# A two-block transformer kernel on one core: norms by a diagonal product, modulation shared by two engines, a three-pass recurrent output, and expert weights in longer rows

## The chip, the core and the metric

The kernel is one program on one core of a Trainium2 chip. TensorE multiplies (PE in the profile; PEld is its weight load), VectorE (DVE), ScalarE (ACT) and GpSimd (POOL) work on tiles, and SyncE (SP) issues the loads. The metric is the device time of one execution in microseconds; less is better.

## The reference

Two blocks run one after the other on 256 tokens of width 1024, beside a context of 256 tokens, all in float32. The first block has an attention layer and a recurrent layer (HGRN2), each followed by a gated feed-forward network (FFN) with a convolution of width 3. The second has dilated and windowed attention and a mixture of 32 experts. What the change touches:

```python
hx = rms_norm(x, norm1_g[layer]) * (1.0 + sc1) + sh1          # before each mixer, with scale and shift from c
x = x + g1 * yx
hx2 = rms_norm(x, norm2_g[layer]) * (1.0 + sc2) + sh2          # before each FFN
# HGRN2: projections q, forget gates fw and bw, input, gate of 8 heads of 128
q = silu(q);  f = lb + (1 - lb) * sigmoid(fl)
o = rms_norm(o_fw + o_bw, o_gain) * silu(gate)                 # the norm is over the 128 of each head
y = o @ w_out
# experts
hdn = gt * sigmoid(1.702 * gt) * (up + 1.0);  y_e = hdn @ w_down[e] + b_down[e]
```

## The kernel before, in words

Tokens lie on partitions in four tiles of 128: tiles 0 and 1 are x, tiles 2 and 3 the context. The residual stream is `xr`. A projection needs its input turned, with the 1024 channels on partitions in 8 chunks, in `hT` and its like.

**Passes.** A float32 product on TensorE is slow. So most products are made in three passes of a faster float type: input and weights are each split in a high part (rounded, by a ScalarE copy) and a low part (the rest, by a VectorE subtraction), and high x high, low x high and high x low are summed in one bank. Two products were still plain float32: the first half of the recurrent queries, `("hq", 0)`, by `move`, and the recurrent output projection `wo1`, by `project`.

**Order of the work.** Each engine runs its own program in the order in which it is written. `psum_ready` counts finished banks; a list (`add`, from line 349 on) fixes in which order the 8 banks are used and whether ScalarE or VectorE empties each. `bank` (TensorE) waits until the reader of the bank eight groups earlier has freed it; `take` (ScalarE, VectorE) waits for the bank. After every ScalarE or VectorE instruction `do` waits for it. `await_next` waits for the next count of a semaphore. SyncE loads weights in units of 2 MB into a ring of three slots, in the order of a list (line 858), each unit after its slot's last user. Slot 2 is also used as scratch, so some units may use slots 0 and 1 only.

**Passage into the first FFN.** `enter_first` (VectorE) adds the projected tile to `xr` by `gated_add` (L2060, L2061), then `rms` makes square sum (L1984), reciprocal (L1988, after ScalarE's square root L1470) and the normed tile `xn` (L1989). TensorE turns it (`turn`, L936). ScalarE modulates the 8 chunks of 128 columns (`norm_turn`, L1490) into `modp` and copies them rounded to `hT_high` (L1494), and VectorE subtracts (`split_tokens`, L2067). The FFN's products wait for all low parts. Weights are rounded by `weights_high` (L1555) and their low part made by `low_part` (L809). The first bank of the FFN is read at L1571.

**Passage into the recurrent layer.** After the last `gated_add` of the FFN, `rms` runs over four tiles, ScalarE modulates all of them into `hT` (`norm_turn`, L1490) and copies the whole to `hx_high` (L1732). VectorE makes the forget gates' lower bounds (L2317 to L2326) and `hx_low` (L2328). The 20 half units of 256 columns follow: `half_high` (L1756) rounds one, VectorE makes its low part (L2350), TensorE uses it, `take_half` empties the banks. `log_forget` (L1780) takes logarithms; `keys_and_sums` (L2335, L2341, L2344) makes running sums. `context_decay` (L1798) and `decay_keys` (L2359) begin the recurrence.

**Recurrence and readout.** For each direction d and half of the heads b, seven levels run through subtraction (VectorE, L2367), exponentials (ScalarE, L1840, L1841), scaling (VectorE, L2388, L2389), products (TensorE) and masks. The last of four passes is (1, 1). Its output is added to `ro` (L2420). Then head norms (L2425 to L2431) run over both tiles of 1024 columns, with the gain row and the gate `rg` multiplied in, then `turn`, ScalarE copies to `hT` (L1504), `wo1` in float32, `gated_add`, and the second FFN, entered as above but with two tiles only, and with its weights rounded after them.

**Experts.** A load of an expert's weight is split in two runs of 2 MB, 16 KB a partition each. Gate, up and down weights have one buffer each; `gate` of expert e+1 is issued when `gate` of e has been multiplied, and so on (L760, L768, L773). Expert 0 is loaded ahead. GpSimd reorders the tokens once (L815) to fit the channels that each partition gets.

## Time and profile before

| | us |
|---|---|
| median of 3 runs | 2708.53 (2706.02 to 2712.92) |
| profiled execution | 2706.67 |
| its span | 2704.8 |
| busy: TensorE, VectorE, ScalarE | 2398.8, 976.9, 787.2 |

The chain of work that ended last is 72% TensorE, 12% DMA, 7% VectorE and 6% ScalarE of the span. A busy time is the sum of an engine's instructions and says nothing of what they wait for; the chain names at each moment what the rest waited for. In the rows below times are microseconds from the start of the span, and a number after x is a count.

### The profile page before, as it was taken

To read this page: it belongs to the slowest core of one execution; us is meant where nothing else is said; L and a number is where in the kernel's file an instruction comes from. 1 tells how busy PE (TensorE), PEld (TensorE's weight loads), DVE (VectorE), ACT (ScalarE), POOL (GpSimd) and SP (SyncE) were. 2 spreads that over 40 slices of the span, in tenths; PEclk is the share of its full clock that TensorE was granted. 3 is DMA by queue.
4 is the path that set the end of the run, shared out by engine and by line. 5 is a ranking of instruction groups with operands and counts; after the bars stand their busy time and mean duration, and the time that the engine had idled before them with its cause. 6 is when DMAs were issued, how large, how long until landed. Compare 5 with 4: busy or idle time off the path is not lost.

```text
span 2704.8 us, 32119 instructions
## 1 busy us (share of the span) xinstructions
PE 2398.8 (89%) x13052; PEld 1574.8 (58%) x13052; DVE 976.9 (36%) x1557; ACT 787.2 (29%) x1242; POOL 4.2 (0%) x6
## 2 busy tenths in 40 slices
PE   6998879999979976579999888799999999999995
PEld 4844857886768966459889873434333333333332
DVE  5465433433332677646543442511111111111112
ACT  4376342322152544235434440110111111011110
POOL 0000000000000000000000000000000000000000
PEclk9999989999979988789999979799999999999998
DMA  8267135322023200225554302699999999999993
GB/s 321 94 233 234 63 109 184 97 94 94 25 96 108 100 1 1 94 89 180 192 190 164 123 1 83 276 424 429 427 429 428 424 430 421 427 429 417 421 429 146
DMA packets 142267, 603.57 MB, mean 223 GB/s; under 512 B 6513, under 2 KB 51825, under 8 KB 117457
## 3 DMA queue, kind: packets, MB, share of 16 engines
q1 hardware_dynamic: 142160, 602.10, 56.8%
q8 instruction: 74, 1.21, 0.2%
q14 instruction: 33, 0.26, 0.0%
HBM read 601.03 MB, written 1.05 MB: 223 GB/s over the span
## 4 chain that ended last, share of the span: by engine, by line
PE 72%; DMA 12%; DVE 7%; ACT 6%; issue 2%; SPq 0%; ACTq 0%; DVEq 0%
PE bank L902 70%; DMA arena<-in_b_up 10%; DMA ring<-in_ada_w 2%; DVE arena L2399 1%; ACT modp L1490 1%; PE bank L936 1%; ACT arena L1718 1%; ACT hT L1490 1%; ACT arena L1527 1%; PE bank L1119 0%; DVE modp L2389 0%; DVE xn L2388 0%; DVE xr L2061 0%; DVE xn L1984 0%; ACT modp L1465 0%
## 5 line engine op out<-in xcount | busy, mean ns | idle before, releaser
L902 PE MATMUL bank<-arena 128*64 128x512 f32 (+5 forms) x2896 | 601.2, 511 | 88.7 <-ACT arena L1934 25.7
L902 PEld LDWEIGHTS bank<-arena 128*64 128x64 f32 (+2 forms) x2896 | 287.6, 169 | 347.4 <-issue 260.7
L902 PE MATMUL bank<-ring,arena 128*64 128x512 f32 (+1 forms) x1632 | 394.9, 608 | 23.7 <-DMA arena<-in_b_up 21.3
L902 PE MATMUL bank<-hT_high,w_split 128*128 128x512 f32 (+1 forms) x1408 | 349.0, 339 | 18.2 <-issue 9.9
L902 PEld LDWEIGHTS bank<-ring,arena 128*64 128x64 f32 (+1 forms) x1632 | 141.0, 143 | 270.3 <-issue 260.1
L902 PEld LDWEIGHTS bank<-hT_high,w_split 128*128 128x128 f32 x1408 | 244.1, 191 | 47.8 <-issue 11.3
L902 PE MATMUL bank<-hT_low,w_split 128*128 128x512 f32 (+1 forms) x704 | 237.9, 338 | 0.0
L2536 DVE TENSOR_SCALAR arena<-bank 128x512 f32<-128x512 f32 x32 | 22.1, 692 | 548.8 <-PE bank L902 548.8
L902 PEld LDWEIGHTS bank<-hT_low,w_split 128*128 128x128 f32 x704 | 134.8, 192 | 14.5 <-issue 1.0
L809 DVE TENSOR_TENSOR w_split<-ring,w_split 128x1024 fp32r<-128x1024 f32 x88 | 107.8, 1225 | 27.6 <-ACT w_split L1555 25.9
L1555 ACT ACTIVATE w_split<-ring 128x1024 fp32r<-128x1024 f32 x88 | 93.4, 1062 | 62.5 <-PE bank L902 49.0
L2540 DVE TENSOR_SCALAR arena<-bank 128x512 f32<-128x512 f32 x32 | 22.1, 692 | 223.2 <-PE bank L902 223.2
L902 PE MATMUL bank<-ring,hT 128*128 128x512 f32 (+1 forms) x240 | 98.1, 570 | 2.9 <-ACTq L720 2.9
L1930 ACT ACTIVATE arena<-arena 128x512 f32<-128x512 f32 x32 | 20.1, 629 | 245.9 <-DVE arena L2536 245.9
L1937 ACT ACTIVATE arena<-bank 128x512 f32<-128x512 f32 x32 | 19.1, 597 | 232.6 <-PE bank L902 232.6
L902 PE MATMUL bank<-down_high,hid_high 128*128 128x512 f32 x216 | 84.9, 393 | 0.0
L902 PE MATMUL bank<-down_low,hid_high 128*128 128x512 f32 x216 | 84.0, 389 | 0.0
L902 PE MATMUL bank<-down_high,hid_low 128*128 128x512 f32 x216 | 84.0, 389 | 0.0
L1921 ACT ACTIVATE arena<-bank 128x512 f32<-128x512 f32 x34 | 18.5, 595 | 208.4 <-PE bank L902 208.4
L902 PEld LDWEIGHTS bank<-ring,hT 128*128 128x128 f32 x240 | 44.5, 197 | 55.2 <-issue 51.3
L2350 DVE TENSOR_TENSOR hw_low<-ring,hw_high 128x2048 fp32r<-128x2048 f32 x18 | 41.3, 2293 | 96.7 <-ACT hw_high L1756 96.6
L902 PE MATMUL bank<-ring,cT 128*32 128x512 f32 x384 | 52.7, 672 | 24.1 <-DMA ring<-in_ada_w 24.1
(344 smaller groups left out, 3671.7 us busy)
## 6 DMA issues: line engine op xcount, KB each, us to landing
ring<-in_w_gate SPq DMA_DIRECT2D x64, 2048.0 KB
arena<-in_w_down SPq DMA_DIRECT2D x64, 2048.0 KB, 15.0
ring<-in_w_up SPq DMA_DIRECT2D x32, 2048.0 KB
arena<-in_w_up SPq DMA_DIRECT2D x32, 2048.0 KB
ring<-in_ada_w SPq DMA_DIRECT2D x24, 2048.0 KB, 8.1
ring<-in_ffn_w_up SPq DMA_DIRECT2D x44, 1024.0 KB, 7.9
ring<-in_w_in SPq DMA_DIRECT2D x11, 2048.0 KB, 7.9
ring<-in_ffn_w_down SPq DMA_DIRECT2D x10, 2048.0 KB, 7.7
```

What stands on the lines that cost most here:

```text
L809: then(eng.tensor_tensor(w[:, 1, :, g, :], raw, w[:, 0, :, g, :].bitcast(F32), ALU.subtract))
L902: return pe.matmul(o, l, r, start=start, stop=stop)
L936: m = pe.transpose(ps[:, i * P:(i + 1) * P], src(t)[:, k * P:(k + 1) * P], ident)
L1490: do(act.activation(o, ps[:, j * P:(j + 1) * P], ACT.Identity, bias=modT[:, l, 24 * i + k, v:v + 1], scale=coef[:, l, i, k, v:v + 1]), F i ...
L1527: do(act.activation(pr, pr, ACT.Exp, bias=st[:, 4 + r:5 + r], accum_out=st[:, 12 + r:13 + r]))
L1555: do(act.activation(w_split[fc % 2][:, 0, :, g, :], raw[:, :, g, fc % 2, :], ACT.Copy), w_high)
L1718: do(act.activation(PT0[:, c % 2, :], ps[:, :], ACT.Copy), F)
L1930: act.activation(sg[:, :], hm[:, :], ACT.Sigmoid, scale=1.702).then_inc(sg_ready, 1)
L2350: do(TT(hw_low[:, slot_of[unit_no[key]], :, 256 * z:256 * z + 256], raw, hw_high[j % 2][:, :, :].bitcast(F32), ALU.subtract), hw_low_ready)
L2399: do(dve.copy_predicated(rA[:, t, :, :], m, ps), F)
L2536: dve.tensor_scalar(hm[:, :], PS[0][:, :], 7.0, None, ALU.min).then_inc(hm_ready, 1)
L2540: link(dve.tensor_scalar(um[:, :], PS[1][:, :], 7.0, -7.0, ALU.min, ALU.max))
```

## The change

1. **Norms by matmul with a diagonal.** `rms` is gone. ScalarE squares and sums a tile itself (`square_sum`) and takes the root; VectorE makes the reciprocal and a 128 x 128 diagonal matrix with it (`inverse_norm`, in the dead rope table). TensorE multiplies `xr` by the diagonal (`pair`, float32), which turns and scales in one product. The products of two tiles stand side by side, 256 columns of one chunk.
2. **Pairs modulated by two engines.** `split_pair`: banks q = 0, 2 are modulated by ScalarE, q = 1, 3 by VectorE, in calls of 256 columns; ScalarE rounds, VectorE makes the low parts. On entry to an FFN, the first products wait for low parts chunk by chunk. In `enter_first` two tiles go together; in the second FFN all weights of the first two columns are rounded before the pair.
3. **Recurrent layer.** The first query half joins the three-pass halves; `("h1", 1)` is turned after the first of them. In ScalarE's loop a half is rounded one iteration later (`half_high(j + 1)` instead of `j + 2`). Norms of tiles 0 and 1 come before the last adds. The lower bounds are made at the start. The gain row is multiplied into `rg` ahead of the recurrence.
4. **Head norms head by head.** ScalarE squares 128 columns at a time with a sum, the first four heads inside pass (1, 1). VectorE scales four heads at a time.
5. **`wo1` in three passes**, with weights rounded inside pass (1, 1), and low parts after the readout.
6. **Expert loads.** Gate and up are each one load of 4 MB, 32 KB a partition, with the token order to fit.

```diff
+            def pair(tag, v):
+                for t in range(2 * v, 2 * v + 2):
+                    await_next(xn_ready)
+                for q in range(4):
+                    key = ("pair", tag, v, q)
+                    ps = bank(key)
+                    for c in range(2):
+                        k = 2 * q + c
+                        for t in range(2 * v, 2 * v + 2):
+                            m = mm(ps[:, c * SEQ + t % 2 * P:c * SEQ + t % 2 * P + P], xr[:, t, k * P:(k + 1) * P],
+                                   diag[:, t, :], True, True)
+                    close(m, key)
...
-                await_next(x_low, 2 * T)
+                x_before = 8 if l else 0
...
+                                if j == 0 and i == 0 and g == 0 and n % 6 == 0:
+                                    pe.wait_ge(x_low, x_before + 2 * T - 4 + k // 2 + 1)
...
                 for t in ALL:
...
+                    if b and t == 3:
+                        pair(("f", 0), 0)
+                    project_split("wo0", b, t, wo_high, o_high, o_low, wo_low_ready)
+            pair(("f", 0), 1)
             ffn(0, NT)
...
-            turn("h1", ALL, lambda t: xn[:, t % 2, :], lambda t: await_next(xn_ready))
-            await_next(hT_ready)
-            s = unit(("hq", 0))
-            for i in range(4):
-                m = move(("hq", i), s, i * P, P, SEQ)
-            release(m)
-            await_next(hx_low_ready)
+            pair("h1", 0)
             for j, (key, z) in enumerate(HALVES):
+                if j == 1:
+                    pair("h1", 1)
                 s = unit(key) if z == 0 else slot_of[unit_no[key]]
                 await_next(hw_low_ready)
+                pe.wait_ge(hx_low_ready, 4 if j < 2 else 8)
...
# ScalarE
+            def square_sum(t):
+                await_next(res_ready)
+                do(act.activation(xn[:, 1, :], xr[:, t, :], ACT.Square, accum_out=stat[:, t:t + 1]))
+                do(act.activation(stat[:, t:t + 1], stat[:, t:t + 1], ACT.Sqrt, bias=C("eps6")[:, 0:1], scale=1.0 / D),
+                   std_ready)
...
+            def split_pair(tag, v, l, i, high, high_sem, low_sem):
+                tok = slice(v * SEQ, (v + 1) * SEQ)
+                for q in range(4):
+                    n = lows[low_sem.name] = lows.get(low_sem.name, -1) + 1
+                    if q % 2 == 0:
+                        ps = take(("pair", tag, v, q))
+                        if n >= 2:
+                            act.wait_ge(low_sem, n - 1)
+                        for c in range(2):
+                            k, cut = 2 * q + c, slice(c * SEQ, (c + 1) * SEQ)
+                            do(act.activation(modp[:, 0, cut], ps[:, cut], ACT.Identity,
                                               bias=modT[:, l, 24 * i + k, v:v + 1], scale=coef[:, l, i, k, v:v + 1]),
+                               F if c else act_step)
+                    else:
+                        await_next(mod_ready)
+                    do(act.activation(high[:, 2 * q:2 * q + 2, tok],
+                                      modp[:, q % 2, :].rearrange("p (k c) -> p k c", k=2), ACT.Copy), high_sem)
...
+            await_next(coef_ready)
+            square_sum(0)
+            square_sum(1)
+            pe_past(("down", 0, NT - 1, 1))
             half_high(0)
+            split_pair("h1", 0, 1, 0, hx_high, hx_high_ready, hx_low_ready)
+            square_sum(2)
+            square_sum(3)
             half_high(1)
-            take_queries(0, 4)
-            await_next(lb_ready)
             for j in range(len(HALVES)):
-                if j + 2 < len(HALVES):
-                    half_high(j + 2)
+                if j and j + 1 < len(HALVES):
+                    half_high(j + 1)
                 take_half(j)
+                if j == 0:
+                    split_pair("h1", 1, 1, 0, hx_high, hx_high_ready, hx_low_ready)
                 if j in LOGS:
                     log_forget(*LOGS[j])
...
+                        if (d, b) == (1, 1):
+                            if n in (1, 2):
+                                head_squares(0, n - 1)
+                            if n >= 4:
+                                wo1_part(n - 4)
...
# VectorE
+            def inverse_norm(t):
+                await_next(std_ready)
+                do(dve.reciprocal(stat[:, t:t + 1], stat[:, t:t + 1]))
+                do(dve.tensor_scalar(diag[:, t, :], ident, stat[:, t:t + 1], None, ALU.mult), xn_ready)
...
                 for t in range(T):
+                    if l == 0 and t == 2:
+                        inverse_norm(0)
+                        inverse_norm(1)
                     for h in range(2):
                         gated_add(("down", l, t, h), h, t, GATE[(l, 1)])
...
             keys_and_sums(1, 1)
+            for t in XS:
+                await_next(rg_ready, 2)
+            for t in XS:
+                v = rg[:, t, :].rearrange("p (h c) -> p h c", h=HG)
+                do(TT(v, v, ROW("og").unsqueeze(1).broadcast_to((P, HG, P)), ALU.mult))
...
+            normed(0)
+            normed(1)
+            for h in range(2):
+                for t in XS:
+                    cut = (slice(None), slice(4 * h, 4 * h + 4), slice(t * P, (t + 1) * P))
+                    ps = take(("turn", "o1", t, h))[:, :].rearrange("p (k q) -> p k q", k=4)
+                    await_next(o1_high_ready)
+                    do(TT(o1_low[cut], ps, o1_high[cut].bitcast(F32), ALU.subtract), F)
+                    signal(o1_low_ready)
+            for j in range(4):
+                wo1_rest(j)
             ffn(1, XT)
...
# SyncE, expert loads
             for j in range(2):
                 slot_free(j)
-                sp.dma_start(moe_slot[j], runs(a["w_gate_2"], e, j)).then_inc(gate_landed, 16)
+            sp.dma_start(ring[:, 0:2, :].rearrange("p a b -> p (a b)"), whole(a["w_gate_2"], e)).then_inc(gate_landed, 16)
...
-                sp.dma_start(moe_slot[2 + j], runs(a["w_up_2"], e, j)).then_inc(up_landed, 16)
+            sp.dma_start(up_w[:, :, :].rearrange("p a b -> p (a b)"), whole(a["w_up_2"], e)).then_inc(up_landed, 16)
```

`head_squares(b, t)` is four Squares of 128 columns with a sum; `wo1_part(j)` a rounding copy of 128 x 2048; `wo1_rest(j)` its low part; `normed(b)` a reciprocal and two products of 512 columns for each of two tiles.

## Rows read from the trace of the kernel before

**Rows 1.** The page: busy times, and two lines of the 40 slices

```profile
PE 2398.8 (89%) x13052; PEld 1574.8 (58%) x13052; DVE 976.9 (36%) x1557; ACT 787.2 (29%) x1242; POOL 4.2 (0%) x6
...
DMA  8267135322023200225554302699999999999993
```

**Rows 2.** Windows: length, busy (count) by engine, granted clock, DMA share, GB/s

```profile
745.00:757.00 12.00, 7.84 (x32) 6.27 (x32) 7.71 (x16) 4.51 (x12) 0.00 (x0) 0.50 1.05 389
...
770.00:775.00 5.00, 5.00 (x15) 4.07 (x16) 0.00 (x0) 4.94 (x4) 0.00 (x0) 0.62 0.00 0
...
1213.00:1217.00 4.00, 4.00 (x35) 4.00 (x35) 3.26 (x5) 2.40 (x3) 0.00 (x0) 1.00 1.09 365
...
1740.00:2656.00 916.00, 867.33 (x4154) 349.06 (x4152) 127.70 (x266) 100.51 (x155) 0.00 (x0) 0.99 1.00 425
```

**Rows 3.** Chain of waits, 275 to 390 us: start, length, what

```profile
287.45 34.82 PE bank L902 x288
...
356.57 0.70 DVE hT_low L2067
```

**Rows 4.** Groups of ScalarE and VectorE, 318 to 358 us: busy, mean ns, idle before

```profile
L1490 ACT ACTIVATE modp<-bank,modT,coef 128x128 f32<-128x128 f32 x32 | 14.6, 458 | 1.1
L1494 ACT ACTIVATE hT_high<-modp 128x512 fp32r<-128x512 f32 x8 | 5.0, 630 | 0.3
...
L2067 DVE TENSOR_TENSOR hT_low<-modp,hT_high 128x512 fp32r<-128x512 f32 x8 | 5.5, 692 | 14.3 <-ACT hT_high L1494 14.3
```

**Rows 5.** Timeline, single instructions of four stretches: start, length, engine, line

```profile
16.74 1.28 ACT L1470 ACT_TABLE_LOAD   x1 [13.40 <-DMA rows<-in_rows]
18.04 1.27 ACT L1470 ACTIVATE stat<-stat,const 128x1 f32<-128x1 f32 x4
...
142.72 0.19 ACT L1709 ACTIVATION_READ_ACCUMULATOR arena<-arena,stat 128x1 f32 x1
...
364.76 0.78 ACT L1571 ACTIVATE xn<-bank,cols 128x512 f32<-128x512 f32 x1 [6.11 <-PE bank L902]
...
2007.57 3.84 PE L902 MATMUL bank<-arena,xn 128*128 128x128 f32 x32
```

**Rows 6.** Timeline of SyncE's issues and of ScalarE, 716 to 812 us

```profile
740.55 89.22 SPq L858 DMA_DIRECT2D ring<-in_hgrn_w_in  x5
...
753.99 15.69 ACT L1490 ACTIVATE hT<-bank,modT,coef 128x128 f32<-128x128 f32 x32
...
785.92 0.38 ACT L1739 ACTIVATE arena<-bank 128x256 f32<-128x256 f32 x1 [3.07 <-PE bank L902]
```

**Rows 7.** DMA issues by line: count, KB each, median us from issue to landing

```profile
ring<-in_hgrn_w_in SPq DMA_DIRECT2D x10, 2048.0 KB, 7.9
```

**Rows 8.** Timeline of VectorE and ScalarE, 880 to 992 us

```profile
913.16 3.36 ACT L1780 ACTIVATE xr<-arena,stat 128x512 f32<-128x512 f32 x4
...
923.23 2.29 DVE L2350 TENSOR_TENSOR hw_low<-ring,hw_high 128x2048 fp32r<-128x2048 f32 x1
...
947.24 2.30 DVE L2335 TENSOR_SCALAR hT<-hT,stat 128x512 f32<-128x512 f32 x4
...
955.38 0.17 DVE L2344 COPY stat<-last_sums 128x4 f32<-128x4 f32 x1
...
959.86 1.22 DVE L2359 TENSOR_TENSOR xr<-xr,arena 128x1024 f32<-128x1024 f32 x1 [0.93 <-ACT xr L1798]
```

**Rows 9.** Timeline of VectorE, ScalarE, and the chain's projection, 1069 to 1205 us

```profile
1097.11 0.69 DVE L2388 TENSOR_TENSOR xn<-arena,xn 128x512 f32<-128x512 f32 x1 [2.50 <-ACT xn L1841]
...
1123.84 0.69 DVE L2420 TENSOR_TENSOR arena<-arena,bank 128x512 f32<-128x512 f32 x1 [1.21 <-PE bank L902]
...
1144.36 30.16 PE bank L902 x64
...
1191.09 4.33 ACT L1555 ACTIVATE w_split<-ring 128x1024 fp32r<-128x1024 f32 x4
1198.31 0.56 ACT L1571 ACTIVATE xn<-bank,cols 128x256 f32<-128x256 f32 x1 [2.90 <-PE bank L902]
```

More of the change, by code:

```diff
@@ L536, in program @@
                     add(("ro", d, b, t), "dve" if d else "act")
-        plan_turn("o1", XS)
+        for h in range(2):
+            for t in XS:
+                add(("turn", "o1", t, h), "dve")
         for b in range(2):
@@ L999, in ffn @@
                 if l:
-                    turn(("f", l), range(T), lambda t: xn[:, t % 2, :], lambda t: await_next(xn_ready))
-                await_next(x_low, 2 * T)
+                    pair(("f", l), 0)
+                x_before = 8 if l else 0
                 for j in range(FC // 2):
@@ L1557, in ffn @@
             def ffn(l, T):
[L1558 to L1563 removed]
+                enter(l)
                 n = T * P
```

345 lines of the change are left out of this document (201 added, 144 removed).

## The prediction

> **What bounds the kernel now.** I read the page first: its busy times, and the DMA line of its 40 slices [rows 1]. TensorE is busy 89% of the span, but DMA is at 9 tenths or more from slice 27 on, so two regimes follow one another. The windows say what rules the second [rows 2]: from 1740 to 2656 us the DMA share is 1.00 at 425 GB/s, which is the expert stage (expert 0 was loaded ahead, 31 experts of 12.6 MB follow). The other two windows give the same stream at shorter rows. So the expert stage costs its bytes; what is saved ahead of it arrives undiminished at the end, since its clock starts with the first gate product, and nothing saved on TensorE inside it would count. The first regime (0 to 1725 us) I read by the chain of waits. It runs along TensorE except at the passages between blocks, where it goes from VectorE to ScalarE and back: 322.4 to 357.3 us [rows 3], 740 to 786 us [rows 6], and 1123.8 to 1198 us [rows 9]. The change sits in these three, in the end of the recurrent projection [rows 8] and in the expert loads.
>
> **Prices of the new operations.** ScalarE modulates 128 columns in 0.458 us now [rows 4]; 512 columns of the same form take 0.78 us [rows 5], so 256 lie between, by the line 0.57 us. The rounding copy is 0.63 us and the low part 0.69 us [rows 4]. A norm by diagonal is 16 f32 products of 128 columns; the same shape in the expert stage, 16 products recorded as x32, takes 3.84 us [rows 5] at full clock. At the other level, 0.50 in the 745 to 757 window [rows 2], it would be up to twice that. VectorE's modulation of 256 columns I take at 0.5 us (bounds 0.35 and 0.69, half and whole of a 512-column operation [rows 4]). A Square with its sum is shown nowhere: 1.08 us for a 1024-column ScalarE pass (4.33 for four [rows 9]) plus the accumulator read, 0.19 and its gap [rows 5], gives 1.35, and 0.57 at 128 columns; bounds 0.6 (a 512-column pass) and 2.6 (with a table load of 1.28 [rows 5] before it).
> One pair of tiles then goes as follows, T being the first bank: ScalarE q0 2 x 0.6 + 0.65 = 1.85; copy of q1 to 2.5; low parts of q0, q1 at 2.7 and 3.4; q2 may start at 2.7; low parts of q2, q3 at 5.3 and 6.0. So 6 us for a pair, where before ScalarE alone took 32 x 0.458 + 8 x 0.63 = 19.7 us for four tiles [rows 4], 9.8 for two.
>
> **Passage 1, attention to the first FFN.** Before: the last low part ends at 357.3 and the first FFN product follows; its first bank closes at 364.7 [rows 3, 5]. After: pair 0 is put in front of the last projection tile on TensorE (done before at about 335.5, behind the other transposes), so that tile ends near 337.4, 3.84 us of pair against the transposes it replaces. VectorE by then has pair 0 and the weights' low part behind it and adds the tile to 339.1. Square and Sqrt to 340.8, diagonal to 341.3, first bank 342.3, low parts at 345.0, 345.7, 347.6 and 348.3. The first FFN bank may now start at the first low part and waits chunk by chunk, so it is bound by the last low part plus six products: it closes at 352.5 (351 if nothing stalls, 354 if the pair runs at the low clock). Gain 12 us (10.5 to 13.5). Queued behind the new waits on TensorE is only the FFN itself.
>
> **Passage 2, FFN to the recurrent projection.** Before: after the adds VectorE makes four norms in turn, then 15.7 us of modulation, then a copy; TensorE starts the first query half at 769.8 and has done with it at 785.9 [rows 6]. After: Square and Sqrt of tiles 0 and 1 run beside the adds, but VectorE waits some 2 us for them in between, so its adds end near 744.8, 4 us after TensorE's last product. New is a wait ahead of everything on ScalarE: the first query weights, issued at 740.6 and landing 7.9 to 8.1 us later [rows 6, 7], hold `half_high(0)` to 748.8, and pair 0's modulation queues behind it. The pair's norm product at 740.4 is hidden by that. Rounding to 750.7, VectorE's low part of the weights (2.29 us [rows 8]) to 753.1, then q1, so the last low part comes at 758.1. The first half, 48 products of 256 columns at 34.82 / 288 = 0.12 us [rows 3], is 5.8 us, plus 1.9 because the clock stands at its lower level after the idle time and rises late (0.62 over the 5 us from 770 [rows 2], 0.38 x 5 = 1.9), to 765.7; pair 1's norm 3.8 to 769.6, the second query half 5.8 to 775.4. Beside it pair 1 ends at 772.7, and ScalarE's next weights only then: 773.9, low part 776.2. The first forget-gate product thus starts at 776.2 instead of 785.9: gain 9.5 us (6 to 12).
>
> **End of the projection.** Two things speak against the change here. The weights' rounding is now ordered behind the previous half's evacuation, and behind the logarithms (3.36 us, after a table load [rows 8, 5]): the last half but two is rounded 1.2 + 1.3 + 3.4 = 5.9 us later. VectorE's keys and sums (947.2 to 955.5, 8.2 us a group) wait for it in order, and its chain that ended at 955.5 ends at 957.0 on the old time scale. Then the gain row multiplied into the gate, 2 x 1.25 = 2.5 us, stands before the first decay. `decay_keys`, at 959.86 now released by ScalarE's exponentials [rows 8], starts at 962.7: 3 us lost (0 to 5).
>
> **Last recurrent pass and readout.** Squares of the first heads (4 x 0.57 = 2.3 us of ScalarE each tile) and four weight roundings (1.95 us each) enter a pass in which VectorE at one place waits 2.5 us for ScalarE [rows 9]. The second squares delay the scaling at 1097.1 by 0.6 us; the second to fourth roundings make ScalarE late by another 1.0. Lost 1.6 us (0 to 4).
> Then the readout. Before: second add 1124.5, norm chain to 1139.8, transposes, f32 projection 30.2 us from 1144.4, adds to 1176.0, norms, modulation of two tiles to 1191.1, four weight roundings, FFN from 1193.6, its first bank at 1198.3 [rows 9]. After, with the 1.6 in it: add to 1126.2; first half of heads scaled by 1129.3, second by 1132.4; transposes beside them; low parts to 1135.7; four weights' low parts at 2.3 each follow in order, the first two by 1138.0 and 1140.3. TensorE: 192 products of 256 columns at 0.12 us = 23.1, from 1138.0, plus 1.9 for the clock = 1163.0 (before 1174.5). Add to 1164.6, Square and Sqrt 1166.3; the four roundings of up weights (4.33 [rows 9]) now stand BEFORE the modulation on ScalarE: 1170.6. VectorE comes from their low parts at 1172.4; low parts of the pair 1174.0 to 1177.4; first FFN bank 1178.8. The low parts of the weights, before after the pair, are then paid. Gain of the whole: 1198.3 - 1178.8 = 19.5 us, the 1.6 counted (14 to 23).
> The forget gates' lower bounds, moved to the start, hide there: ScalarE waits 13.4 us for the first parameters [rows 5], and the moved exponential with its table load is 1.5 us.
>
> **Expert loads.** Gate and up come as one 4 MB load of 32 KB rows instead of two of 16 KB. Order and releases stay: the product waited for all loads of its weight already, and all three of expert 0 are issued together. Only bytes per second can change. From the windows [rows 2] a row costs an engine 44.9 ns (1 KB, 365 GB/s), 84.2 (2 KB, 389), 617 (16 KB, 425): a line with 6 to 8 ns per row. One less per 32 KB is 0.45 to 0.66% on two thirds of 916 us: 2.8 to 4 us. I take 3.5; bounds 0 and, the other way, rival 3. The Trainium skill (DMA: Bandwidth & Descriptors, "Where 436 GB/s comes from") puts the ceiling of the ports at 435 GB/s. If all of the distance from 425 to 435 were cost per row, 16 KB would take 602 ns and 15 more, and the estimate by that page would be 7 us instead of 3.5. The 1 and 2 KB windows give half of those 15 ns at most, so the rows decide.
>
> **Sum.** 12 + 9.5 - 3 + 19.5 + 3.5 = 41.5. Some thirty handoffs of about 0.07 us that the timelines leave out take back 2: gain 39.5. The profiled execution took 2706.7 us (span 2704.8); the median of the runs is 2708.5, 1.8 above it. 2706.7 - 39.5 = 2667.2, or 2669 by the median; I say 2668.
>
> **Rivals.**
> 1. The stream does not notice the longer rows: 3.5 less, 2671.5. For it: 425 is the mean with dips, and the line rests on windows of a few us. It differs too little to be told from the forecast by the total, only by the stage.
> 2. The shared modulation ping-pongs: each half of `modp` is single, so ScalarE waits for VectorE's low part and VectorE for ScalarE's copy. If a pair costs what it did (9.8 us, not 6), three pairs on the path cost 3 x 3.8 = 11.4, and if half of the readout's gain goes the same way (the four weights' low parts wait behind everything on VectorE), 8 more (half of 19.5 - 3.8): 2667.2 + 19.4 = 2687. For it: VectorE's idle before each low part, 14.3 us in eight, is of this kind [rows 4]. Against: VectorE now carries half of the modulation.
> 3. Slower than before: rows at a 32 KB pitch make the 16 DMA engines collide. All 16 read addresses 128 KB apart instead of 64. At the 2 KB windows' 389 GB/s the 260 MB of gate and up would take 668 instead of 611 us: +57, less 36 for the rest (39.5 without the 3.5): 2667.2 + 3.5 + 57 = 2728. It decides from 6% loss of rate on, 425 to 400 GB/s. No row shows pitch as a cost: the 1 and 2 KB rows come at pitches of 20 to 22 KB and lie on the line.
> 4. Squares between exponentials call for their own table: two extra loads of 1.28 us in each of two places, about half hidden: +2.5. For it: no row shows a Square between exponentials. Against: it is the only kind of ScalarE work here that would. The Trainium skill (ScalarE: Activation LUTs, "What ACT_TABLE_LOAD costs") adds a drain of about 1.4 us to every switch; this trace does not show it, the Sqrt at 18.04 starts 0.02 us after its load's end [rows 5], and with the rule the rival would cost twice as much. It lies inside my range.
>
> **How the numbers follow.** Forecast with rivals 1 and 4 in it, 72%, itself 2660 to 2677; rival 2, 17%; still better than forecast, because the first FFN banks hide more, 6%; rival 3 or another loss of that size, 3%; other losses 2%. Leaving out a tenth at each end: 2655 to 2688. About 0.3% (8 us) is what a measurement can tell. Faster 0.95, same 0.02, slower 0.03.
>
> **What would show it.** Right: first FFN product near 345 and first bank by 354; ScalarE idle to the landing of the first query weights and the first forget product about 21 us earlier than 785.9; VectorE going into `decay_keys` without a wait for ScalarE; projection with 192 products of 0.12 us; 31 experts in 912 us at 427 GB/s. Wrong: low parts more than 7 us after a pair's first bank, table loads among the squares, DMA share below 1.00 or under 420 GB/s in the expert stage.

## The result and the profile after

The changed kernel takes 2666.12 us (median of 4 runs, 2664.47 to 2668.32) against 2709.27 us (4 runs, 2706.02 to 2712.92) of the kernel before: ratio 0.984, 95% interval 0.9828 to 0.9852, 43 us or 1.6% faster. I had said 2668 (2655 to 2688). The page after, in its rows that answer to [rows 1]:

```profile
span 2662.6 us, 32524 instructions
PE 2390.5 (90%) x13292; PEld 1587.2 (60%) x13292; DVE 984.0 (37%) x1574; ACT 792.6 (30%) x1247; POOL 4.2 (0%) x6
...
PEclk9999999999989988899999898899999999999997
...
DMA packets 133053, 603.61 MB, mean 227 GB/s; under 512 B 5488, under 2 KB 50800, under 8 KB 116432
```

The busy times have hardly moved (TensorE -8, VectorE +7, ScalarE +5 us): what went is idle time between engines, and the lower clock that follows it. So the page can't say where; stages can. I cut each trace at landmarks that all kernels have (a bank's first read, a product, a load). "Others" are the traces of the experiments below in which that stage is not edited; a stage is timed from its own first landmark. The first stage holds a small edit: the forget gates' lower bounds stand there now.

| stage, us | before (others) | changed (others) | gain | forecast |
|---|---|---|---|---|
| start to first add of the attention's projection | 293.7 (294.8 to 299.7) | 296.0 (294.3 to 301.5) | -2.3 | 0 |
| passage 1, to the first FFN bank read | 71.1 (71.0 to 71.5) | 60.4 (60.1 to 60.5) | 10.7 | 12 |
| first FFN, to its first down add | 366.4 | 366.4 | 0 | 0 |
| passage 2 and projection, to its last bank read | 224.6 (224.6 to 225.5) | 217.3 (217.3 to 217.9) | 7.3 | 9.5 |
| to the first decay product | 4.1 | 7.8 | -3.6 | -3 |
| four recurrent passes | 155.2 (154.5 to 155.5) | 154.4 (156.0 to 157.2) | 0.8 | -1.6 |
| readout, to the second FFN's first bank | 83.3 (83.2 to 83.3) | 62.6 (62.7) | 20.6 | 21.1 |
| second FFN, to its last gate bank read | 120.9 | 120.9 | 0 | 0 |
| its down products, second attention, router, to expert 1's gate load | 420.3 (420.3) | 415.2 (407.7 to 421.5) | 5.0 | 0 |
| experts, to the end | 965.3 (964.4, 965.5) | 961.6 (959.7 to 961.9) | 3.7 | 3.5 |
| sum | | | 42.2 | 41.5, less 2 for handoffs |

The sum is right to 3 us, but that closeness is partly luck: 5 us of it come from a stage that the change doesn't touch, and the first stage, 2.3 us longer in this trace, lies within its scatter in the others. The rows that carry the stages follow; times are start and duration, the bracket is the idle time before and what ended it.

Passage 1, timeline of ScalarE, VectorE, ScalarE again, and TensorE's norm products of the first and the second pair (answers to [rows 3 to 5]):

```profile
320.50 1.06 ACT L1533 ACTIVATE xn<-xr 128x1024 f32<-128x1024 f32 x1 [27.48 <-DVEq L743]
321.47 0.18 ACT L1533 ACTIVATION_READ_ACCUMULATOR xn<-xr 128x1 f32 x1
321.67 1.28 ACT L1534 ACT_TABLE_LOAD   x1
322.96 0.30 ACT L1534 ACTIVATE stat<-stat,const 128x1 f32<-128x1 f32 x1
...
343.89 0.29 DVE L2079 TENSOR_SCALAR rope<-const,stat 128x128 f32<-128x128 f32 x1
348.14 1.12 DVE L2089 TENSOR_SCALAR modp<-bank,coef,modT 128x256 f32<-128x256 f32 x2 [3.97 <-PE bank L929]
352.15 1.42 DVE L2095 TENSOR_TENSOR hT_low<-modp,hT_high 128x512 fp32r<-128x512 f32 x2 [0.16 <-ACT hT_high L1555]
...
346.41 1.16 ACT L1550 ACTIVATE modp<-bank,modT,coef 128x256 f32<-128x256 f32 x2 [2.83 <-PE bank L929]
356.34 0.78 ACT L1633 ACTIVATE xn<-bank,cols 128x512 f32<-128x512 f32 x1 [1.37 <-PE bank L929]
...
330.18 3.74 PE L929 MATMUL bank<-rope,xr 128*128 128x128 f32 x32
...
344.27 6.49 PE L929 MATMUL bank<-rope,xr 128*128 128x128 f32 x32 [4.61 <-DVE rope L2079]
```

The new prices are close to the forecast: a Square with its sum takes 1.17 us from its start to the next instruction (1.35 forecast), 256 columns 0.58 on ScalarE (0.57) and 0.56 on VectorE (0.5). The Square comes ahead of the table load and needs none. From the diagonal (343.89) the pair takes 9.7 us to its last low part at 353.57 (352.15 + 1.42). TensorE's 16 norm products, recorded as x32, took 3.74 us for the first pair and 6.49 for the second, which stands behind 4.61 us of idle time.

Passage 2, chain of waits (start, duration, what), and VectorE's low part of the weights that the first forget-gate product needs (answers to [rows 6, 7]):

```profile
732.14 7.83 DMA ring<-in_hgrn_w_in
...
740.07 1.92 ACT hw_high L1814
742.01 2.30 DVE hw_low L2456
...
749.08 0.70 DVE hx_low L2095
...
750.03 17.97 PE bank L929 x128
768.00 1.66 issue
```
```profile
767.27 2.29 DVE L2456 TENSOR_TENSOR hw_low<-ring,hw_high 128x2048 fp32r<-128x2048 f32 x1 [1.25 <-ACT hw_high L1814]
```

The chain calls the last 1.66 us "issue", time in which it sees no wait. But the forget-gate product starts at 769.66, 0.10 us after that low part ends (769.56), and the program makes it wait for it.

End of the projection, timelines of ScalarE and VectorE (answers to [rows 8]):

```profile
917.62 3.36 ACT L1839 ACTIVATE ring<-hT,stat 128x512 f32<-128x512 f32 x4
921.01 1.92 ACT L1814 ACTIVATE hw_high<-ring 128x2048 fp32r<-128x2048 f32 x1
...
923.03 2.29 DVE L2456 TENSOR_TENSOR hw_low<-ring,hw_high 128x2048 fp32r<-128x2048 f32 x1 [1.62 <-ACT hw_high L1814]
942.04 2.48 DVE L2493 TENSOR_TENSOR arena<-arena,rows 128x1024 f32<-128x1024 f32 x2
947.79 1.23 DVE L2498 TENSOR_TENSOR xr<-xr,arena 128x1024 f32<-128x1024 f32 x1
```

Readout, chain of waits (answers to [rows 9]):

```profile
1120.06 0.70 DVE o_low L2587
1120.90 2.31 DVE hw_low L2577
1123.45 25.34 PE bank L929 x192
...
1150.39 1.16 ACT xn L1533 x2
1151.89 1.06 ACT w_split L1622
1153.05 1.24 DVE w_split L836
...
1162.32 0.70 DVE hT_low L2095
```

### The profile page after: what moved, and what is told of

Its sections match the earlier page's. It is cut to its first block, busy times and chain, and to the rows that moved or that the text cites. A ratio compares the mean times of both kernels' runs of the same rounds, so it can differ in the third digit from the quotient of the medians.

```text
span 2662.6 us, 32524 instructions
## 1 busy us (share of the span) xinstructions
PE 2390.5 (90%) x13292; PEld 1587.2 (60%) x13292; DVE 984.0 (37%) x1574; ACT 792.6 (30%) x1247; POOL 4.2 (0%) x6
## 2 busy tenths in 40 slices
DMA packets 133053, 603.61 MB, mean 227 GB/s; under 512 B 5488, under 2 KB 50800, under 8 KB 116432
## 4 chain that ended last, share of the span: by engine, by line
PE 73%; DMA 12%; DVE 7%; ACT 5%; issue 2%; SPq 0%; ACTq 0%; DVEq 0%
PE bank L929 72%; DMA arena<-in_b_up 10%; DMA ring<-in_ada_w 1%; DVE arena L2538 1%; ACT arena L1781 1%; DMA ring<-in_attn_w_in 0%; ACT arena L1586 0%; PE bank L963 0%; PE bank L1182 0%; ACT arena L2030 0%; ACT modp L1522 0%; ACT w_split L1622 0%; DVE xn L2527 0%; DVE modp L2528 0%; PE bank L1441 0%
## 5 line engine op out<-in xcount | busy, mean ns | idle before, releaser
L929 PE MATMUL bank<-arena 128*64 128x512 f32 (+6 forms) x2384 | 479.3, 491 | 92.5 <-ACT arena L2030 25.7
L929 PEld LDWEIGHTS bank<-arena 128*64 128x64 f32 (+2 forms) x2384 | 240.7, 172 | 281.0 <-issue 190.7
L929 PE MATMUL bank<-ring,arena 128*64 128x512 f32 (+1 forms) x1120 | 269.5, 596 | 1.2 <-DMA arena<-in_b_gate 0.3
L929 PE MATMUL bank<-up_w,arena 128*64 128x512 f32 x1024 | 235.0, 613 | 19.3 <-DMA arena<-in_b_up 19.3
L929 PEld LDWEIGHTS bank<-ring,arena 128*64 128x64 f32 (+1 forms) x1120 | 101.5, 142 | 163.5 <-issue 154.3
L929 PEld LDWEIGHTS bank<-up_w,arena 128*64 128x64 f32 x1024 | 79.0, 140 | 174.0 <-issue 174.0
L929 PE MATMUL bank<-hx_high,hw_high 128*128 128x512 f32 (+1 forms) x192 | 69.5, 362 | 16.0 <-DVE hx_low L2095 14.3
```

What stands on the lines that cost most here:

```text
L929: return pe.matmul(o, l, r, start=start, stop=stop)
```

## Experiments

Each is timed against the kernel before on its own chip, whose medians there lie between 2708.9 and 2709.9 us; differences to the changed kernel's median compare runs made at different times and on several chips. For effects of a few us the stages of one trace each decide, since totals carry the spread of the first and the untouched stages. All edits are to the changed kernel unless said otherwise.

**rows16 and before_rows32: the expert loads alone, taken away and added.**

```
-            sp.dma_start(ring[:, 0:2, :]..., whole(a["w_gate_2"], e)).then_inc(gate_landed, 16)
+                sp.dma_start(moe_slot[j], runs(a["w_gate_2"], e, j)).then_inc(gate_landed, 16)
```

> The changed kernel, with the expert loads of gate and up back at two runs of 16 KB rows each (and the tokens in the order that goes with them). The profiled execution of the changed kernel takes 961.6 us from the issue of expert 1's gate to its end, the kernel before 965.3. Theory (each DMA engine pays 6 to 8 ns per row): this kernel returns to 965.1 us (964.5 to 965.8), all 16 KB windows at 425 GB/s, and nothing ahead of the expert stage moves; total 3.5 us above the changed kernel. Rival (the stream does not notice the longer rows, and the 3.7 us between the two kernels are scatter): 961.6 within 1 us.

> The kernel before, with nothing but the expert loads of gate and up as one run of 32 KB rows each. From the issue of expert 1's gate to the end it took 965.3 and 964.4 us in two traces with 16 KB rows, 964.4 in the changed kernel with 16 KB rows, and 959.7 to 961.6 in seven traces with 32 KB rows. Theory (the rows alone do it): 960.4 us (959.5 to 961.7), and all stages ahead as in the kernel before; total 4.4 us less. Rival (it needs the rest of the change, the order or the phase in which the stage is entered): 964 to 965.5.

Windows over the expert stage of the kernel before, the changed kernel, rows16 and before_rows32 (after the length: busy times and instructions of the five engines, granted clock, DMA share, GB/s):

```profile
1739.47:2704.80 965.33, 889.73 (x4260) 359.19 (x4256) 145.74 (x292) 104.66 (x162) 0.00 (x0) 0.98 0.96 406
```
```profile
1701.01:2662.60 961.59, 889.59 (x4260) 358.36 (x4256) 145.69 (x292) 104.67 (x162) 0.00 (x0) 0.98 0.95 407
```
```profile
1706.06:2670.50 964.44, 889.73 (x4260) 359.20 (x4256) 145.71 (x292) 104.66 (x162) 0.00 (x0) 0.98 0.96 406
```
```profile
1744.22:2704.50 960.28, 887.85 (x4260) 358.14 (x4256) 145.70 (x292) 104.65 (x162) 0.00 (x0) 0.98 0.95 408
```

16 KB rows: 964.4 to 965.5 in four traces of three kernels; 32 KB rows: 959.7 to 961.9 in ten traces. Both ways, and with everything else of the change or nothing, the longer rows bring the gain: 4.3 us between the means (964.9 and 960.6). 31 experts have 2 x 128 rows fewer each, 496 for each of 16 engines: 8.6 ns per row if all of it is theirs, above my 6 to 8. But the loads are halved with the rows. The page of the kernel before has

```profile
DMA packets 142267, 603.57 MB, mean 223 GB/s; under 512 B 6513, under 2 KB 51825, under 8 KB 117457
```

against 133053 and 5488 after: besides the 32 x 256 rows some 1020 packets under 512 B are gone, 16 for each load saved. What belongs to the row and what to the load no run separates. Totals: rows16 2671.46 (ratio 0.9855, 0.9835 to 0.9875); before_rows32 2705.13 against 2709.89 (0.998, 0.9969 to 0.9991).

**wo1_f32: the readout's projection without three passes.**

```
-                    project_split("wo1", b, t, wo1_high, o1_high, o1_low, wo1_low_ready)
+            await_next(hT_ready)
+            project("wo1", XS)
```

> The changed kernel, with the recurrent output projected in plain float32 from transposed heads, as before, and without the eight roundings and low parts that three passes need; head norms, norm by diagonal and shared modulation stay. In the changed kernel TensorE starts the projection at 1123.5, 3.4 us after its last operand low part, because the weights' first low part stands in between, runs 25.3 us, and the first FFN bank is read at 1164.9. Theory (the passes themselves bring little, the readout's gain of 20.6 us is the shorter chain of norms): start at about 1120.0, 30.2 us as before, end at 1150.2 against 1148.8, so the first FFN bank 1.4 us later (0 to 3), total +1.4. Rival (the three passes bring what their products save and more, since the roundings lie in free time): 5 us later or more.

Its chain of waits:

```profile
1120.22 0.60 ACT hT L1949
1120.92 30.33 PE bank L929 x64
```

From the last pass to the FFN bank 64.96 instead of 62.64: 2.3 us, in the theory's bounds; the rival falls. Of the readout's 20.6 us the three passes are worth 2.3; the other 18.3 are the shorter chain of norms and its order, the wait by chunk (wait_all, below) among them. And the 2.3 are not all profit, because the weights' roundings stand in the pass ahead. The last pass alone, in the kernel before, in wo1_f32 (squares, no roundings) and in rows16 (squares and roundings), with the lower clock at the same place of the pass in all three:

```profile
1074.49:1115.06 40.57, 28.53 (x200) 26.86 (x200) 30.29 (x37) 15.75 (x31) 0.00 (x0) 0.88 0.45 155
```
```profile
1061.51:1102.15 40.64, 28.60 (x200) 26.93 (x200) 30.29 (x38) 18.98 (x48) 0.00 (x0) 0.88 0.46 156
```
```profile
1068.26:1110.17 41.91, 28.56 (x200) 26.89 (x200) 30.29 (x38) 26.58 (x52) 0.00 (x0) 0.88 0.44 151
```

With roundings and this clock it takes 41.8 to 41.9 in six traces. So the squares cost nothing there and the roundings 1.2 us, and the three passes bring about 1.1 net, where the theory had 1.4. In the changed kernel's own trace, filler and weights_early the roundings are there too, but the pass has some 5 us less at the lower clock and takes 40.6. (Total 2660.88, ratio 0.9827, 0.9809 to 0.9845, lower than the changed kernel's although the edited stage is longer: its second attention and router took 407.7 instead of 415.2, see below.)

**one_engine: ScalarE modulates all chunks.**

```
-                    if q % 2 == 0:
-                        ps = take(("pair", tag, v, q))
+                    ps = take(("pair", tag, v, q))
...
-                        do(dve.tensor_scalar(modp[:, 1, cut], ps[:, cut], coef[:, l, i, k, v:v + 1],
```

> The changed kernel, with ScalarE modulating all eight chunks of every tile pair; VectorE only makes the low parts. Theory (two engines at once are what shortens a pair): ScalarE needs 4 x (1.16 + 0.63) = 7.2 us for a pair and the last low part comes 8 us after the first bank instead of 6, so about 1.8 us later at each of four places (both pairs ahead of the first FFN, the first ahead of the recurrent projection) and 0.6 at the readout, where ScalarE is held by weights anyway: total +5 us (3 to 7.5), of which +3.5 at the first FFN bank (356.3 in the changed kernel). Rival (VectorE is what a pair waits for, with 1.12 us of modulation and two low parts of 0.69 for two chunk pairs): nothing lost, total within 1 us.

Passage 1 took 62.4 (+2.0), passage 2 with the projection 219.9 (+2.6), the readout 63.4 (+0.7): 5.3 us, as the theory's sum, though passage 1 has less of it (2.0 where I had 3.5) and passage 2 more. Total 2673.86, ratio 0.9868 (0.9843 to 0.9894), +7.7.

**wait_all: the first FFN product waits for every low part.**

```
-                                if j == 0 and i == 0 and g == 0 and n % 6 == 0:
-                                    pe.wait_ge(x_low, x_before + 2 * T - 4 + k // 2 + 1)
+                                if j == 0 and i == 0 and g == 0 and n == 0:
+                                    pe.wait_ge(x_low, x_before + 2 * T)
```

> The changed kernel, with the first FFN product waiting for all low parts of its activations at both FFN entries, instead of chunk by chunk. In the changed kernel the last low part ends at 353.6 and the first bank is read at 356.3; at the second FFN 1163.7 and 1164.9. Theory: all 24 products now stand behind the last low part: 24 x 0.24 = 5.8 us of 512 columns and 24 x 0.12 = 2.9 of 256, so the banks are read at 359.5 (+3.2) and 1166.8 (+1.9) on the changed kernel's scale, more by up to 2 us each if TensorE's idle time takes its clock down. Total +5 (4.5 to 9). Rival (other waits of the first banks cover it, such as the convolution's chain or the weights): under 2 us in total.

Passage 1 64.9 (+4.5), readout 67.3 (+4.6), total 2675.1, ratio 0.9876 (0.9859 to 0.9894): +9.0, the upper end. That is more than the products behind the last low part (3.2 and 1.9 expected): the lower clock lasts 10.2 instead of 6.8 us in the one and 27.3 instead of 20.5 in the other. Waiting by chunk is worth a fifth of the whole change.

**order and gain_late: the two causes of the late decay product.**

```
+                if j == 1:
+                    half_high(2)
-                if j and j + 1 < len(HALVES):
-                    half_high(j + 1)
+                if j and j + 2 < len(HALVES):
+                    half_high(j + 2)
```
```
                             sub(d, b, n + 1)
+                        if (d, b, n) == (0, 1, 0):
+                            for t in XS:
+                                v = rg[:, t, :].rearrange("p (h c) -> p h c", h=HG)
+                                do(TT(v, v, ROW("og").unsqueeze(1).broadcast_to((P, HG, P)), ALU.mult))
...
-            for t in XS:
-                v = rg[:, t, :].rearrange("p (h c) -> p h c", h=HG)
-                do(TT(v, v, ROW("og").unsqueeze(1).broadcast_to((P, HG, P)), ALU.mult))
```

> The changed kernel, with ScalarE in the recurrent projection again rounding half j+2 ahead of its evacuation of half j (from j = 1 on), instead of half j+1. In the changed kernel VectorE comes to the gain row 2.0 us after the last projection bank is read and to the first decay product 7.8 us after it (4.1 in the kernel before). Theory (the roundings ordered behind the logarithms hold VectorE's keys and sums back): the gain row starts 0.2 us before that read, the decay product 5.6 us after it, 2.2 us gained there and nothing elsewhere. Rival (the gain row's 2.5 us are all that counts, VectorE catches up by itself): 7.8 as before, nothing gained.

> The changed kernel, with the multiplication of the gain row into the gates (2 x 1.25 us of VectorE) moved from ahead of the first decay product into the first level of the second recurrent pass, where VectorE sits idle for 5 us. Theory: first decay product 5.3 us after the last projection bank is read instead of 7.8, and the second pass as long as it was, total 2.5 us less. Rival (ScalarE's exponentials hold the decay product, as in the kernel before): not under 7 us, and nothing gained.

VectorE in order, where the last bank is read at 942.40, and in gain_late, where that is 938.14:

```profile
942.26 2.48 DVE L2495 TENSOR_TENSOR arena<-arena,rows 128x1024 f32<-128x1024 f32 x2
948.01 1.23 DVE L2500 TENSOR_TENSOR xr<-xr,arena 128x1024 f32<-128x1024 f32 x1
```
```profile
943.39 1.22 DVE L2493 TENSOR_TENSOR xr<-xr,arena 128x1024 f32<-128x1024 f32 x1
```

5.6 and 5.25 us after the read, as expected to 0.1 us: each cause costs 2.2 to 2.5 where both stand. In gain_late the four passes take 156.2 us, within the spread of the others, so the gain row is free where it is now. Totals 2661.24 (0.9819, 0.9802 to 0.9835) and 2660.78 (0.9821, 0.9805 to 0.9837), 5 below the changed kernel; 3 of these are again the untouched second attention and router (412.3 instead of 415.2 in both).

**filler: products without use in the readout's gaps.**

```
+            def fill(key, n):
+                ps = bank(key)
+                for _ in range(n):
+                    mm(ps[:, 0:P], ident, ident, True, True)
```

> The changed kernel, with 12, 4 and 8 products of 128 columns whose results are overwritten, put on TensorE where it waits in the readout: ahead of the first and second half of the heads' transposes and ahead of the projection (waits of 4.1, 1.8 and 4.3 us). In the changed kernel the granted clock is 0.50 from 1114.8 to 1128.1, after those waits began at 1109.9, and the projection from 1123.45 takes 25.34 us where 192 x 0.12 = 23.0. Theory (the fall of the clock follows TensorE's idle time): no fall, projection 23.1 us, first FFN bank 2.3 us earlier. Rival (the clock falls all the same, or the fillers' own time delays the transposes): nothing gained, or up to 2 us lost.

The granted clock in the changed kernel just after its projection began, and in filler, whose projection began at 1129.69:

```profile
1124.00:1126.00 2.00, 2.00 (x12) 2.00 (x11) 1.97 (x2) 0.00 (x0) 0.00 (x0) 0.50 0.00 0
```
```profile
1130.00:1132.00 2.00, 2.00 (x15) 2.00 (x14) 1.97 (x2) 0.00 (x0) 0.00 (x0) 0.74 0.00 0
1132.00:1134.00 2.00, 2.00 (x11) 2.00 (x11) 2.00 (x1) 0.00 (x0) 0.00 (x0) 0.50 0.01 4
```

The lower level in the stage went from 20.5 to 10.2 us, so it does follow idle time. But most of what went had lain in the waits: 3.4 us of idle time were left after the last filler, and within the projection the lower level still lasted 3.4 us instead of 4.7. It took 24.76 us instead of 25.34. Stage 62.06, 0.6 us gained instead of 2.3; total 2668.48, ratio 0.985 (0.9833 to 0.9866). Time at the lower level costs only where TensorE has work in it.

**before_again and before_delay: where 5 us come from that nobody edited.**

> The kernel before once more, for its trace. In its first trace the way from the last gate bank of the second FFN to the last exponential of the second attention takes 288.1 us, in that of the changed kernel 283.1, though no instruction in between differs; the lower clock level lasts 14 us less there. Theory (where the lower level falls in that stretch depends on chance and on its phase, not on the change): this trace differs from 288.1 by more than 2 us, or the changed kernel's variants spread as widely, which four of them do already (279.6, 282.1, 283.1 and 288.5). Rival (the kernel before always has the long one): 288.1 within 1 us.

The rival held: 288.1, and 77.67 us from the first to the last exponential, to 0.01 us as in the first trace, so scatter from run to run it is not (total of this one run 2707.0). But one_engine had 78.0 with the change in it. What could be tried on the kernel before was a shift of the work ahead of the stage:

```
                             ps = bank(key)
+                            if l == 1 and j == 5 and i == 0 and g == 0:
+                                for n in (P, P, P, P, P, 64):
+                                    mm(ps[:, 0:n], ident, ident[:, 0:n], True, True)
```

> The kernel before, with 1.3 us of TensorE work added in the middle of the second FFN (five products of 128 columns and one of 64 ahead of a gate bank, overwritten afterwards). From the first to the last exponential of the second attention three traces of the kernel before took 77.66, 77.67 and 77.67 us, the changed kernel and five of its variants 71.4, three others 67.9, 69.2 and 78.0, without a differing instruction in the stretch; what differs is where TensorE's lower clock level falls. Theory (the level falls by the position at which the stage is entered, and the changed kernel has merely come to another position): shifted by 1.3 us the kernel before takes 71.4 there too, and 1.3 us more each in the FFN and on the way to the first exponential, so added work makes it 3.7 us shorter, 2706 against 2709.9. Rival (the stage is 6.3 us shorter because of something that the change does, memory contents or semaphores left over): 77.67 again, total 1.3 us longer.

The same 346 products, from the first to the last exponential of the second attention, in the kernel before, before_delay, the changed kernel and one_engine:

```profile
1529.64:1607.30 77.66, 66.35 (x346) 54.08 (x346) 47.36 (x142) 44.60 (x142) 0.00 (x0) 0.80 0.08 28
```
```profile
1537.77:1613.18 75.41, 64.67 (x346) 53.11 (x346) 47.35 (x142) 44.54 (x142) 0.00 (x0) 0.82 0.08 29
```
```profile
1497.48:1568.89 71.41, 60.44 (x346) 49.60 (x346) 47.35 (x142) 44.59 (x141) 0.00 (x0) 0.88 0.09 30
```
```profile
1501.68:1579.70 78.02, 67.30 (x346) 55.70 (x346) 47.34 (x142) 44.55 (x142) 0.00 (x0) 0.78 0.08 28
```

75.41, not the 71.4 that I expected, but no longer 77.67; the router behind it fell from 132.2 to 128.7. With the added 1.3 us in the FFN the way from there to expert 1's gate went from 420.3 to 415.5, and the total from 2709.84 to 2706.81 (ratio 0.999, 0.9981 to 1.0): adding work did not make the kernel slower, and the untouched stages are 4.8 us shorter, the size of what the changed kernel gets there. VectorE and ScalarE are busy for the same time in all four rows; TensorE's busy time follows the clock. So a stage's length is not fixed by its own code, and added work ahead of it changes it without anything of the change.

It is not the time in the span that decides: two traces of the kernel before and that of before_rows32 read the last gate bank of the second FFN at 1319.2, 1320.4 and 1323.9 us and take 77.66 to 77.67. What the shift moved is where the clock's falls lie against the work. Counted from that read, the first fall comes after 215.7 to 215.8 us in those three, but after 67.7 in before_delay, and after 67.6 to 67.7 in the changed kernel, rows16, order and gain_late. The three us from 67.8 on, in the kernel before, before_delay and the changed kernel:

```profile
1387.01:1390.01 3.00, 1.66 (x16) 1.42 (x13) 2.54 (x2) 2.39 (x4) 0.00 (x0) 1.00 1.03 392
```
```profile
1394.13:1397.13 3.00, 3.00 (x16) 2.85 (x14) 2.54 (x2) 1.70 (x3) 0.00 (x0) 0.50 1.04 395
```
```profile
1353.57:1356.57 3.00, 3.00 (x15) 3.00 (x16) 2.28 (x2) 1.32 (x3) 0.00 (x0) 0.50 1.03 394
```

Which shift gives which length I can't say beforehand; one shift was tried.

**weights_early and best: a version from what the traces showed.** best is order, gain_late and weights_early together; of weights_early the added lines (those that they replace are left out):

```
                 if l:
+                    weights_high(l, 0)
+                    weights_high(l, 1)
                 square_sum(0)
...
+                weights_low(1, 0)
+                weights_low(1, 1)
                 for t in XS:
                     add_tile("wo1", 1, t, GATE[(1, 0)])
...
+                    if (d, b) == (1, 1):
+                        wo1_rest(0)
+                        wo1_rest(1)
```

> The changed kernel with only the two shifts of the readout: low parts of the first two output weights ahead of the last readout sums, and roundings and low parts of the first up weights during the output projection. Theory: from the last pass to the first FFN bank 57.0 us instead of 62.6 to 62.7, of which 2.3 from an earlier start of the projection and 3.3 after it; stages ahead and the FFN itself unmoved. Rival (the first is spent in the adds or the pass, since VectorE's idle time there is only just long enough, 4.7 for 4.6 us): 59.3.

> The changed kernel with four shifts of order: roundings of the recurrent projection one half earlier (as in the run before), the gain row moved into the second recurrent pass (as in the run before), the low parts of the first two output weights made in VectorE's 4.7 us of idle time ahead of the last readout sums, and the roundings and low parts of the first up weights made during the output projection (both engines wait 4.3 us and more there) instead of between norm and modulation. Theory: the first decay product comes 4.2 us after the last projection bank's read (7.8 in the changed kernel; the two shifts alone gave 5.6 and 5.3, together they meet ScalarE's exponentials); projection from 1121.1 instead of 1123.5; the pair's low parts end 6 us after its first bank, so the first FFN bank is read 57.0 us after the last pass (62.6 to 62.7 now). Sum 3.6 + 2.3 + 3.3 = 9.2 us, so a median near 2657 against 2666. Rival (another wait takes their place: ScalarE's copies or the clock's fall in the shortened passages): half of it or less, 2661 to 2666.

The chain of waits of best, readout, and its norm products in full:

```profile
1122.00 25.03 PE bank L929 x192
...
1150.79 3.77 PE bank L929 x16
```
```profile
1150.79 6.62 PE L929 MATMUL bank<-rope,xr 128*128 128x128 f32 x32 [3.77 <-DVE rope L2079]
```

The stage is 58.1 in both (62.6 in the changed kernel), 4.6 gained instead of 5.6: the projection starts 2.6 us earlier (2.3 expected), and what follows it is 2.0 shorter (3.3 expected). The norm products are on the path now and no weights are, and these products stand almost wholly at the lower clock (0.50 from 1149.9 to 1156.7): 6.62 us, where the changed kernel's took 5.18 behind its own wait. The decay product comes 4.14 us after the read in best, where ScalarE's exponentials hold it as in the kernel before. 8.2 us in stages, then; but the medians are 2661.45 (ratio 0.9816, 0.9801 to 0.9831) and 2664.65 (0.983, 0.9814 to 0.9845). best is faster than the kernel before by 48 us and lies 4.7 below the changed kernel, within overlapping intervals. I had expected 2657; the total lies where the rival had it (2661 to 2666), though the stages show 8.2 of the 9.2 us. 1.3 us came back on the way to the second attention's exponentials; the rest is not told from the spread of the first stage (300.3 in its trace).

## Why the prediction was right, and where it was off

- **Passage 1** (12 forecast, 10.7 measured). Step by step, with the start's 2.3 us put in, the diagonal was due at 343.6 and was ready at 344.2 (343.89 + 0.29). The low parts should have ended at 350.6 and ended at 353.6: the granted clock was 0.50 from 343.1 to 349.9, the pair's norm products took 6.49 us instead of the 3.84 that I had at the upper clock, and VectorE waited 3.97 us for its first bank. I had that only in the bound. My close of the FFN bank was generous by 1.4 us, so half of it was made good.
- **Passage 2** (9.5; 7.3). Through the first pair's last low part all steps hold to 0.4 us: load 7.8, rounding, VectorE's weights, last low part at 749.8 where my 758.1, less the 8.4 gained ahead, gives 749.7. The products behind it took 17.97 instead of 17.3: 5.8 + 3.7 + 5.8 are 15.3, so the clock cost 2.7 where I had 1.9. The forget product then waited for its weights' low part, which I had at 767.8 on this scale and which ended at 769.56, since ScalarE came to the rounding behind the second pair only at 765.25. That is 1.9 us late in all. Another 0.4 is a misreading: 785.9 is ScalarE's read of the last query bank, the first forget product of the kernel before starts at 785.47. Mis-sized terms, in the range of 6 to 12.
- **End of the projection** (-3; -3.6). Mechanism and both prices shown by order and gain_late.
- **Recurrent passes** (-1.6). The one trace says +0.8, but six traces in which no pass is edited have a mean of 156.1 (154.4 to 157.2) against 155.1 in four of before: -1.0. For the last pass alone, where the edit is, wo1_f32 gives the split: I had 0.6 for the squares and 1.0 for the roundings; at the same place of the lower clock it was 0 and 1.2. A square takes 0.44 us a head instead of 0.57.
- **Readout** (21.1 without the passes; 20.6). The sum holds step by step: from the last pass the projection starts after 21.2 us (21.3 forecast) and ends after 46.6 (46.3), and the FFN bank is read after 62.6 (62.1). Norms and order give 18.3 of it and the three passes 2.3, of which their roundings take 1.2 back in the last pass. I had charged the projection 1.9 us for the clock; it was 25.34 - 23.04 = 2.3.
- **The clock, in all three passages**, is the term that I had too small: nothing instead of 2.7 us in passage 1, 1.9 instead of 2.7 in passage 2, 1.9 instead of 2.3 in the readout.
- **Expert loads** (3.5; 4.3 between the means). Rival 1 is refuted from both sides, rival 3 too: from 1702 to 2614 us the DMA share is 1.00 at 428 GB/s. The estimate by the Trainium skill (DMA: Bandwidth & Descriptors, "Where 436 GB/s comes from"), 7 us, is too high by 2.7: the windows' slope was the better guide.
- **Rival 2** (ping-pong): from its first bank's read a pair took 6.3 us at the upper clock (passage 1's first, 331.4 to 337.6) and 7.2 where TensorE was at the lower clock until 349.9 (346.4 to 353.6), far from 9.8. The 7.2 is just over the 7 that I had named as a sign of being wrong; the cause is the clock, not the ping-pong. Without sharing it is 5.3 us more in all.
- **Rival 4**: no table load among squares; the last of the squares that stand between exponentials ends its read at 1077.75, the next exponential starts at 1077.78.
- **What I didn't foresee**: the second attention and router. I took a stage without an edit for a constant. It gave 5 us, by luck in the forecast's favour, and covers the first stage's 2.3 us and 2 us of short terms; without it the forecast would have been 3 us too good, still well inside its range.

## What to carry to other kernels

Compare stage by stage between landmarks that both kernels have, and look at the granted clock of each stage first: a total can move by 5 us in code that nobody touched, in either direction, and an edit of 2 us can't be read from it. Ahead of a matmul phase, let it wait for its operand chunk by chunk (9 us here), and put weight roundings and low parts where both vector engines already wait for TensorE (4.6 us for two such shifts), not between norm and modulation. When a change bundles a new norm and a cheaper matmul, undo one of them before praising either.

## What the hardware showed that I had not expected

- The same stretch with the same 346 products took 67.9 to 78.0 us in fourteen traces, with 3.4 to 34.1 us at the lower clock level in it: 10.15 / 30.7 = 0.33 us lost per us at that level. The value repeats to 0.01 us in the kernel before and before_rows32 (77.66, 77.67, 77.67), and lies at 71.4 in the changed kernel and six of its variants.
- A DMA row costs at most 8.6 ns beside its bytes at 16 to 32 KB, where DMA is busy throughout; a part of that may be the load's.
- The first 300 us spread by 7 us with the same code (294.3 to 301.5 in ten traces of the changed kernel and its variants, 293.7 to 299.7 in four of the kernel before and its variants), from the first modulation banks on.
